# Three weight rings, and all memory behind them, placed 64 bytes higher than the x blocks

## The reference, cut to what matters

```python
p   = x @ w_in                                   # 2048 x 6412
... three groups of heads on p: RWKV-7, retention, mLSTM -> o_rw, o_ret, o_ml
mix = concatenate([o_rw, o_ret, o_ml], -1) @ w_out        # 2048 x 2048
x1  = layernorm(ALPHA * x + mix)
hdn = silu(x1 @ w_gate) * (x1 @ w_up)            # 2048 x 5632 each
x2  = layernorm(ALPHA * x1 + hdn @ w_down)       # 5632 x 2048
```

## The kernel before, in words

| tensor | before | after |
|---|---|---|
| x_hi, x_lo | 192, 18624 | 192, 18624 |
| w_raw, w_hi, w_lo | 37056, 53440, 69824 | 37120, 53504, 69888 |
| arena: o_hi, o_lo | 102784, 119680 | 102848, 119744 |
| arena: h_hi, h_lo | 102784, 149248 | 102848, 149312 |

## Time and profile before

### The profile page before, as it was taken

How to read it: one execution, slowest core, us unless ns; L and a number is a source line. 1 busy time by engine, 2 the same in 40 slices (tenths; PEclk the granted TensorE clock), 3 DMA queues, 4 the chain that set the end, 5 groups by cost and what they waited for, 6 DMA issues and landing times.

```text
span 2776.7 us, 55787 instructions
## 1 busy us (share of the span) xinstructions
PE 2696.8 (97%) x23575; PEld 2620.6 (94%) x23575; DVE 1623.9 (58%) x1769; ACT 1163.6 (42%) x1460; POOL 0.2 (0%) x4
## 2 busy tenths in 40 slices
PE   7999999999999999999999999999999999999997
PEld 7988899899999999999999998987999999999997
DVE  5567457688555545444586574577875545555444
ACT  4445343446333333333354453353553333333332
POOL 0000000000000000000000000000000000000000
PEclk9999999999999999999999999999999999999998
DMA  7544225366666666555564542353666666665553
GB/s 228 171 134 118 88 85 175 101 175 180 181 181 180 180 178 181 178 179 169 181 200 142 176 126 84 88 151 104 185 186 186 176 182 180 181 182 186 194 177 114
DMA packets 280392, 447.37 MB, mean 161 GB/s; under 512 B 45302, under 2 KB 76336, under 8 KB 279928
## 3 DMA queue, kind: packets, MB, share of 16 engines
q1 hardware_dynamic: 278600, 441.59, 52.8%
q10 hardware_dynamic: 1618, 3.21, 0.4%
HBM read 432.97 MB, written 11.78 MB: 160 GB/s over the span
## 4 chain that ended last, share of the span: by engine, by line
PE 88%; DVE 7%; ACT 3%; issue 2%; ACTq 0%; DMA 0%; DVEq 0%; SPq 0%
PE psum L695 19%; PE psum L696 19%; PE psum L697 19%; PE psum L728 6%; PE psum L729 5%; PE psum L730 5%; DVE w_lo L1750 2%; ACT w_hi L1320 1%; PE psum L718 1%; PE psum L719 1%; PE psum L720 1%; PE psum L925 1%; PE psum L1096 1%; PE psum L1081 1%; PE psum L1085 1%
## 5 line engine op out<-in xcount | busy, mean ns | idle before, releaser
L1746 DVE TENSOR_TENSOR w_lo<-w_raw,w_hi 128x1024 fp32r<-128x1024 f32 x496 | 605.8, 1225 | 682.3 <-ACT w_hi L1307 681.2
L1307 ACT ACTIVATE w_hi<-w_raw 128x1024 fp32r<-128x1024 f32 x504 | 533.9, 1061 | 896.7 <-PE psum L697 862.2
L695 PE MATMUL psum<-x_hi,w_lo 128*128 128x264 f32 (+3 forms) x3072 | 877.8, 286 | 2.1 <-DVE x_lo L2073 1.0
L696 PE MATMUL psum<-x_lo,w_hi 128*128 128x264 f32 (+3 forms) x3072 | 875.1, 285 | 0.0
L697 PE MATMUL psum<-x_hi,w_hi 128*128 128x264 f32 (+3 forms) x3072 | 874.5, 285 | 0.0
L695 PEld LDWEIGHTS psum<-x_hi,w_lo 128*128 128x128 f32 x3072 | 579.6, 189 | 3.4 <-issue 1.3
L696 PEld LDWEIGHTS psum<-x_lo,w_hi 128*128 128x128 f32 x3072 | 580.8, 189 | 0.2
L697 PEld LDWEIGHTS psum<-x_hi,w_hi 128*128 128x128 f32 x3072 | 579.8, 189 | 0.0
L1750 DVE TENSOR_TENSOR w_lo<-w_raw,w_hi 128x1024 fp32r<-128x1024 f32 x304 | 368.2, 1222 | 206.6 <-ACT w_hi L1320 189.9
L1320 ACT ACTIVATE w_hi<-w_raw 128x1024 fp32r<-128x1024 f32 x292 | 304.4, 1055 | 290.1 <-PE psum L730 211.7
L728 PE MATMUL psum<-x_hi,w_lo 128*128 128x264 f32 (+1 forms) x1376 | 412.3, 300 | 4.1 <-DVE w_lo L1750 1.4
(11 more groups left out here) (501 smaller groups left out, 2513.8 us busy)
## 6 DMA issues: line engine op xcount, KB each, us to landing
w_raw<-in_w_in SPq DMA_DIRECT2D x192, 512.0 KB, 3.9
w_raw<-in_w_gate SPq DMA_DIRECT2D x176, 512.0 KB, 3.7
w_raw<-in_w_up SPq DMA_DIRECT2D x176, 512.0 KB, 4.1
w_raw<-in_w_down SPq DMA_DIRECT2D x176, 512.0 KB, 4.1
w_raw<-in_w_out SPq DMA_DIRECT2D x64, 512.0 KB, 3.9
w_raw<-in_w_in SPq DMA_DIRECT2D x16, 262.0 KB, 2.8
r_sample<-in_state_ret SPq DMA_DIRECT2D x6, 512.0 KB, 7.7
out_s_ret<-r_sample SPq DMA_DIRECT2D x6, 512.0 KB, 6.7
```

What stands on the lines that cost most here:

```text
L695: mm(out, w1, bh[:, k, 0:nt], start=(k == 0), stop=False)
L696: mm(out, w0, bl[:, k, 0:nt], start=False, stop=False)
L1307: A(wh[:, j, :, :], raw[:, j, :, :], ACT.Copy).then_inc(S.hi_ready, 1)
L1746: TT(wl[:, j, :, :], raw[:, j, :, :], wh[:, j, :, :].bitcast(F32), ALU.subtract).then_inc(S.lo_ready, 1)
```

## The change

Between the x blocks and the first ring, 64 bytes are skipped. Nothing else in the code is different: the same instructions in the same order, with other addresses.

```diff
@@ -136,6 +136,7 @@
     x_at = here[0]
     xh = put("x_hi", [128, KB, XW], F32R)
     xl = put("x_lo", [128, KB, XW], F32R)
+    here[0] += 64
     raw = put("w_raw", [128, RING, 2, GC])
     wh = put("w_hi", [128, RING, 2, GC], F32R)
     wl = put("w_lo", [128, RING, 2, GC], F32R)
```

## The result

The changed kernel takes 2786.74 us in the median of 12 runs (2782.64 to 2791.18), against 2782.51 us in the median of 12 runs of the kernel before (2775.09 to 2785.32). The ratio is 1.0017, with a 95% interval of 1.0009 to 1.0025: slower by 4.7 us, between 2.5 and 7.0. The 4.7 lies inside the 0.2% that were called "same", and the interval leaves no doubt that it is slower. The profiled execution takes 2787.94 us, with a span of 2786.2. Since the diff adds a line, L695 of before is L696 after, and so on.

What follows compares the result with a forecast made beforehand. The prediction took TensorE's matmul pace to bound the kernel. It put +2.8 us for the x blocks, with all other terms at nothing, on a median of 2785.2 us, giving 2788.0 us, range 2774 to 2803.

Steps and rivals of the forecast that it cites:

- same: Whole kernel: a change within about 0.2%, 5.6 us or 5 ns per x block, counts as no change.
- The bound: Whole kernel: TensorE, busy 97% of the span, sets the time by matmul pace; addresses move a block by up to 3%.
- The x blocks: Matmuls reading x: 1112 blocks at new distances 64 and 192 cost 2.5 ns more each, +2.8 us.
- Down and out-projection: Matmuls reading h and o: distances stay, only absolute addresses move by 64 bytes; costed at nothing.
- The doubt about the place in the ring: Blocks at equal distances cost differently, perhaps by place in the ring; priced rows could each be off by 0.02 us.
- what came before: Same unequal costs at equal distances: another possible reason was what preceded the block; rows could be off by 0.02 us.
- The loads: Weight slab loads: 2048-byte rows now start at 0 modulo 256; 0.4 us or less, hidden by the ring, costed at nothing.
- Slower: Every x block: weight and moving reads collide more often at 64 and 192; +14 us, 2799 us, chance 0.32.
- Faster: x blocks: distances of 64 keep the two streams apart, 1.45 us per block; -8 us, 2777 us, chance 0.26.
- The case that nothing depends on addresses: Moving and weight reads don't meet, so the change does nothing; 2785.2 us, included in the forecast's chance 0.42.
- The median: Whole kernel: base to which the sum was added, 2785.2 us, 6.65 us above the profiled execution.
- The forecast of 2788.0: x blocks: costs dealt anew, mean staying within 1.4525 to 1.4625 us; 2788 us, chance 0.42.

Runs made afterwards that it cites:

- e4: Kernel before with the x blocks and everything behind them moved up 64 bytes, so every distance stays; ratio 1.0005 [0.9996, 1.0015].
- e5: Against the kernel before, only x_lo moved by 64 bytes modulo 256; 2780.96 us in one timed execution, beside 2783.05 before.
- e6: Against the kernel before, only x_hi moved by 64 bytes modulo 256; 2780.52 us in one timed execution, beside 2783.05 before.
- e8: Against the kernel before, 32 bytes skipped between x blocks and rings; 2779.56 us in one timed execution, beside 2783.05 before.
- e9: Against the kernel before, x_lo and w_lo both moved by 64 bytes modulo 256; 2775.25 us median, ratio 0.9978 [0.9968, 0.9988].
- e7: Against the kernel before, only the ring w_lo moved by 64 bytes modulo 256; 2784.03 us in one timed execution, beside 2783.05 before.

## Why the prediction was right

**The bound.** It is TensorE's pace, and the pace depends on addresses: both held. One piece of evidence for the second was no effect of addresses: 1.44 against 1.47 us for x blocks 7 and 9 is the alternation of 1444 and 1474 ns, which comes at equal addresses modulo 256 (e4). Everything that the change did to the time of the work itself, it did in the time from one matmul to the next.

**The x blocks.** The term was +2.8 us (2.5 ns on each of 1112 blocks); the measured sum over the x matmuls is +2.8 us. That agreement is luck. The distances of after stand the wrong way round in the prediction (it is 192 for even blocks and 64 for odd ones), which its mean doesn't feel. The step priced all 13344 matmuls by blocks of `product`. In truth the 7872 of `product` with 264 columns became dearer by 0.83 ns each, 10 ns per block, four times what I took, and the other 5472 cheaper by about 0.7 ns each. One mean hid two terms of opposite sign, +6.5 and -3.8 us. The error of the first was in how the three rows were weighed: o block 12 and h block 4 (both 64 in the high part, 1.45 and 1.46 us) stand for one distance and h block 8 (192, 1.47) for the other, and since even and odd blocks are equally many, the mean is (1.455 + 1.47) / 2 = 1.4625, not 1.46: 5 ns per block instead of 2.5. The measured 1456 and 1477 ns fall into those two classes, the dear one 7 ns above its row. e5, e6 and e8 show that this was no rule: the low part and w_lo count as much, and the h rows at steps of 32 bytes didn't carry over to x at all. That h blocks and x blocks agreed at 64 and 192 was worth a bet with a wide range and no more. The row that I had not looked for is `tile`'s, which reads the same data with the same weights in another order.

**Down and out-projection** stayed to the matmul: 944 and 944 records in 115 us of down, 121.55 and 121.64 ns in the out-projection. Absolute addresses don't count (e4). The doubt about the place in the ring was wrong, and the one about "what came before" was right (e4's second layer).

**The loads.** Nothing. ScalarE's largest group of waits for loads comes to 15.2 us after, 14.2 before:

```profile
ACT w_hi L1308 <- DMA w_raw<-in_w_down: 15.2, 7, 5.4
```

And the weights' queue took 52.5% of 16 engines' time in a span of 2786.2 us, 1463 us, where it was 52.8% of 2776.7, 1466 us. That is 0.2% less where the beats of the Trainium skill, page "DMA: Bandwidth & Descriptors", section "How a descriptor splits into AXI transactions", gave an estimate of 9%. For rows of 2048 bytes that start at 192 or at 0 modulo 256, these profiles show no such price.

**The rivals.** Slower had its direction right for the x blocks of `product`, and the dear distance, 192, as well; that the two reads meet more often there is not shown. The mean there is 1466.5 ns, over the 1462.5 from which I had it decide; it did not decide because the other x matmuls took 3.8 us back. Faster, at 1.45 us and 2777 us, didn't come at 64 bytes, but e9 comes near it in the block (1453 to 1454 ns) and to it in the time (2775.25 us). The case that nothing depends on addresses is out: moving w_lo alone took 20 ns off every even x block (e7), with the same instructions on every engine. The Trainium skill, page "SBUF — State Buffer", section "SBUF: two separate sides", gives TensorE an independent port for weight loads; the runs don't show where the two reads meet, only that the pace depends on how far apart they are, modulo 256 bytes.

**The median.** I put the sum on 2785.2 us, the median of three; twelve runs put it at 2782.5, 2.7 us lower. Against that the change measured +4.7 us by the ratio where the sum had +2.8. The forecast of 2788.0 against 2786.7 is close because the two errors, a base too high and a step too small, partly cancel.

## What to carry to other kernels

Where TensorE is at 97% and its matmuls take more than their columns at the granted clock, the placement of the moving tensor against the weights is worth a look: here some bytes skipped between tensors moved the time by -0.2 to +0.3% with no other change. Read it in the time from start to start of neighbouring matmuls, block by block: it repeats to the nanosecond, while a timed run hides it behind stretches of lower clock. Price every instruction stream that reads the moved data by rows of its own order, not by one mean, and if a layout is worth having, run the few candidates, since effects of single tensors didn't add.

## What was not expected of the hardware

In gate and up a matmul with 264 moving columns and 128 columns of weights follows the last after 119.5 to 123.1 ns on average over a block (1434 to 1477 ns per 12), with 110.0 ns for the columns at 2.4 GHz (half of the 220 ns at 1.2 GHz); which it is goes by the distances of x_hi, x_lo, w_hi and w_lo modulo 256 bytes, and with a distance of 128 in all, two blocks at equal addresses modulo 256 take 1444 and 1474 ns in turn. At 1.2 GHz it is 220 ns, the columns alone. Why is not settled: no run here takes the weight loads or the moving reads away, and all that the 220 ns rule out is an addition per matmul that stays the same at both clocks, in time or in cycles. The other surprise is how much the lower clock costs and varies: 31 to 58 us at 1.2 GHz, 14 to 26 us of time at 45% of it, in profiles of kernels whose instructions are all the same. In the twelve runs of the changed kernel the mean granted clock goes from 0.988 (2790.99 and 2791.18 us) to 0.991 (2782.64 us): 0.003 x 2786 / 0.5 = 16.7 us more at 1.2 GHz, by the 45% an estimate of 7.5 us of the 8.5 between the slowest and the fastest.
